# First transfers in quarters, and the last normalisation shared by VectorE, ScalarE and GpSimd with stores in halves

## The reference, cut to what matters

```python
def layer_norm(x, g, b):
    mu = xf.mean(-1, keepdims=True)
    var = jnp.square(xf - mu).mean(-1, keepdims=True)
    return (xf - mu) * lax.rsqrt(var + LN_EPS) * g + b

for l in range(DEPTH):                       # DEPTH = 2
    mix = hybrid_mixer(x, mem, w_in[l], ..., w_mem_kv[l], w_out[l], cos, sin)
    x = layer_norm(DEEPNORM_ALPHA * x + mix, ln1_g[l], ln1_b[l])
    ffn = moe_ffn(x, ...)
    x = layer_norm(DEEPNORM_ALPHA * x + ffn, ln2_g[l], ln2_b[l])

km, vm = jnp.split(mem @ w_mem_kv, 2, axis=-1)   # inside hybrid_mixer
```

## Time and profile before

| | us |
|---|---|
| median of 3 runs | 1241.95 |
| profiled execution, whole time | 1242.17 |
| its span (first to last instruction of the core) | 1240.2 |
| PE busy | 1199.5 |
| DVE busy | 426.9 |
| ACT busy | 335.4 |
| POOL busy | 10.4 |

### The profile page before, as it was taken

The page is one execution under the profiler, slowest core; times in us unless marked ns, Lnnn a source line. Parts: engine busy times, 40 slices in busy tenths (PEclk is TensorE's granted clock), DMA queues, the critical chain, the costliest instruction groups (busy, mean ns, idle before and its releaser), DMA issues.

```text
span 1240.2 us, 18632 instructions
## 1 busy us (share of the span) xinstructions
PE 1199.5 (97%) x8032; PEld 550.5 (44%) x8032; DVE 426.9 (34%) x1198; ACT 335.4 (27%) x637; POOL 10.4 (1%) x20
## 2 busy tenths in 40 slices
PE   7999899999999999999899999999999999999994
PEld 5764443333443334433386645344333443334431
DVE  0433732332333323333334336233333333333335
ACT  0132222322223222233212323222232222322221
POOL 0000000000000000000010000000000000000001
PEclk9999999999999999999999999999999999999998
DMA  9962389999999999999967405899999999999990
GB/s 390 417 282 80 103 358 435 424 435 425 432 424 427 429 432 429 432 426 433 423 248 309 193 35 221 362 429 430 430 433 427 431 429 428 429 429 428 429 400 37
DMA packets 26713, 452.48 MB, mean 365 GB/s; under 512 B 2944, under 2 KB 3072, under 8 KB 5504
## 3 DMA queue, kind: packets, MB, share of 16 engines
q1 hardware_dynamic: 26624, 451.21, 86.1%
HBM read 450.15 MB, written 1.05 MB: 364 GB/s over the span
## 4 chain that ended last, share of the span: by engine, by line
PE 95%; DVE 3%; DMA 1%; ACT 1%; issue 0%; POOL 0%; SPq 0%; POOLq 0%
PE bank L596 36%; PE bank L622 18%; PE bank L517 8%; PE bank L542 7%; PE bank L678 4%; PE bank L750 4%; PE bank L687 2%; PE bank L608 2%; PE bank L877 1%; PE bank L697 1%; PE bank L566 1%; PE bank L707 1%; PE bank L652 1%; PE bank L646 1%; PE bank L529 1%; DMA slots<-in_dense 1%
## 5 line engine op out<-in xcount | busy, mean ns | idle before, releaser
L622 PE MATMUL bank<-slots,scratch 128*32 128x512 f32 x2048 | 233.0, 595 | 2.3 <-issue 2.3
L596 PE MATMUL bank<-slots,xT 128*64 128x512 f32 x1024 | 226.1, 594 | 1.0 <-ACT xT L912 1.0
L596 PE MATMUL bank<-slots,scratch 128*64 128x512 f32 x1024 | 226.0, 594 | 0.0
L1183 DVE SCALAR_TENSOR_TENSOR scratch<-bank,small,scratch 128x512 f32<-128x512 f32 x128 | 96.1, 751 | 248.7 <-ACT scratch L912 248.7
L912 ACT ACTIVATE scratch<-bank,small 128x512 bf16<-128x512 f32 x128 | 87.9, 687 | 159.0 <-PE bank L622 159.0
L912 ACT ACTIVATE scratch<-bank 128x512 f32<-128x512 f32 (+2 forms) x122 | 67.0, 562 | 236.0 <-PE bank L517 76.9
L517 PEld LDWEIGHTS bank<-scratch 128*128 128x128 bf16 x1536 | 107.7, 146 | 50.4 <-issue 49.7
L596 PEld LDWEIGHTS bank<-slots,xT 128*64 128x64 f32 x1024 | 69.3, 137 | 130.6 <-issue 129.3
L596 PEld LDWEIGHTS bank<-slots,scratch 128*64 128x64 f32 x1024 | 69.2, 137 | 129.4 <-issue 129.4
L517 PE MATMUL bank<-scratch 128*128 128x128 bf16 x1536 | 117.1, 227 | 0.3
L622 PEld LDWEIGHTS bank<-slots,scratch 128*32 128x32 f32 x2048 | 60.8, 109 | 121.1 <-issue 117.1
(11 more groups left out here) (125 smaller groups left out, 697.2 us busy)
## 6 DMA issues: line engine op xcount, KB each, us to landing
slots<-in_w_gu SPq DMA_DIRECT2D x64, 4096.0 KB, 22.6
slots<-in_w_dn SPq DMA_DIRECT2D x64, 2048.0 KB, 20.9
slots<-in_dense SPq DMA_DIRECT2D x32, 1024.0 KB, 11.3
r<-in_pool_mat SPq DMA_DIRECT2D x2, 1024.0 KB, 19.7
r<-in_ln_g SPq DMA_DIRECT2D x4, 512.0 KB, 4.5
r<-in_ln_b SPq DMA_DIRECT2D x4, 512.0 KB, 5.9
slots<-in_shared_dn SPq DMA_DIRECT2D x2, 1024.0 KB, 4.9
scratch<-in_memt SPq DMA_DIRECT2D x2, 512.0 KB, 6.8
```

The lines of the kernel that those rows point to most:

```text
L596: m = pe.matmul(H[64 * a:64 * a + 64, :], xg[B % 2][:, k, j, a, :], GU[g][:, a, :, k, :], start=k == 0, stop=k == KD - 1)
L622: m = pe.matmul(Y[half][r0:r0 + 32, :], hT[:, kc * P + 64 * a + 32 * t:kc * P + 64 * a + 32 * t + 32], DN[g][:, a, kc, half * 512:(half + ...
L1183: dve.scalar_tensor_tensor(yres[:, half * 512:(half + 1) * 512], Y[half][:, :], wslot[:, b:b + 1], ysp[:, 0, half * 512:(half + 1) * 512], ...
```

## The change

At the start, the first layer's memory tokens and key and value weights are transferred in four quarters each (rows of 2 KB and of 4 KB), with a semaphore for each quarter. PE waits at k = 0, 2, 4 and 6 instead of at k = 0 and 4. The second layer keeps its halves. The count that PE waits for on later chunks of that buffer is adapted.

At the end, DVE runs the first pass (subtract mean, times gain) over both tiles without a wait for `rstd`. The second pass over tile 1 stays on DVE, in two halves of 512 columns. For tile 0 ScalarE multiplies by `rstd` in two halves, and GpSimd, behind its last `rstd` operation, adds the bias in two halves. SP stores four halves of 256 KB: tile 1's first, then tile 0's.

```diff
-                for h in range(2):
+                for i in range(4 if l == 0 else 0):
+                    a, z = i * KD * S // 4, (i + 1) * KD * S // 4
+                    sp.dma_start(mt[:, a:z], memt[:, a:z]).then_inc(first_in[i], 16)
+                    a, z = i * W_CHUNK // 4, (i + 1) * W_CHUNK // 4
+                    sp.dma_start(r[:, a:z], dense[l, 0][:, a:z]).then_inc(first_in[i], 16)
+                for h in range(2 if l else 0):
...
-            for t in range(NT):
-                sp.wait_ge(*x_at(DEPTH - 1, 1, t))
-                sp.dma_start(out[0, t * P:(t + 1) * P, :], xs[:, t, :]).then_inc(out_done, 16)
-            sp.wait_ge(out_done, 16 * NT)
+            for t in (1, 0):
+                for h in range(2):
+                    sp.wait_ge(out_rd[t], h + 1)
+                    a, z = h * D // 2, (h + 1) * D // 2
+                    sp.dma_start(out[0, t * P:(t + 1) * P, a:z], xs[:, t, a:z]).then_inc(out_done, 16)
+            sp.wait_ge(out_done, 16 * 2 * NT)
...
-                        if j == 0 and k % 4 == 0:
+                        if l == 0 and j == 0 and k % 2 == 0:
+                            pe.wait_ge(first_in[k // 2], 32)
+                        if l and j == 0 and k % 4 == 0:
...
+            act.wait_ge(centred, 1)
+            act.wait_ge(rstd_rd, 4 * DEPTH - 1)
+            for h in range(2):
+                v = xs[:, 0, h * 512:(h + 1) * 512]
+                copy(v, v, scale=rstd[:, 0:1]).then_inc(scaled, 1)
...
-                for t in range(NT):
-                    normalised(l, 1, t)
+                if l < DEPTH - 1:
+                    for t in range(NT):
+                        normalised(l, 1, t)
+                else:
+                    dve.wait_ge(ln_in, 64 * l + 64)
+                    for t in range(NT):
+                        dve.wait_ge(var_rd, 4 * l + 2 + t + 1)
+                        m = dve.scalar_tensor_tensor(xs[:, t, :], xs[:, t, :], mv[:, t, 0:1], lng, ALU.subtract, ALU.mult)
+                        m.then_inc(centred, 1)
+                    dve.wait_ge(rstd_rd, 4 * l + 4)
+                    dve.wait_ge(centred, 2)
+                    for h in range(2):
+                        v = xs[:, 1, h * 512:(h + 1) * 512]
+                        dve.scalar_tensor_tensor(v, v, rstd[:, 1:2], lnb[:, h * 512:(h + 1) * 512], ALU.mult, ALU.add)\
+                            .then_inc(out_rd[1], 1)
...
+            for h in range(2):
+                v = xs[:, 0, h * 512:(h + 1) * 512]
+                pool.wait_ge(scaled, h + 1)
+                pool.tensor_tensor(v, v, lnb[:, h * 512:(h + 1) * 512], ALU.add).then_inc(out_rd[0], 1)
```

More of the change, by code:

```diff
@@ L294, in build @@
         out_done = sem("out_done")
+        first_in = [sem(f"first_in{i}") for i in range(4)]
+        centred = sem("centred")
+        scaled = sem("scaled")
+        out_rd = [sem(f"out_rd{t}") for t in range(NT)]
         class Pass:
@@ L508, in chunk_wait @@
                 for h in halves:
-                    pe.wait_ge(chunk_in[c % 3][h], 48 * l + 16 * (c // 3) + 16)
+                    pe.wait_ge(chunk_in[c % 3][h], 48 * l + 16 * (c // 3) + (16 if c % 3 else 0))
             def gather(ps, B, quarter, buf, to=G):
@@ L642, in _ @@
                     for k in range(KD):
-                        if j == 0 and k % 4 == 0:
+                        if l == 0 and j == 0 and k % 2 == 0:
+                            pe.wait_ge(first_in[k // 2], 32)
+                        if l and j == 0 and k % 4 == 0:
                             chunk_wait(l, 0, (k // 4,))
-                            pe.wait_ge(memt_in[k // 4], 16 * l + 16)
+                            pe.wait_ge(memt_in[k // 4], 16)
                         m = pe.matmul(o[:, j * S:(j + 1) * S], W[0][:, k, j * P:(j + 1) * P], memT[l][:, k, :],
```

## The result

| | before | after |
|---|---|---|
| median of 12 runs, us | 1242.05 | 1246.06 |
| profiled execution, whole time | 1242.17 | 1245.75 |
| its span | 1240.2 | 1243.6 |

The ratio of the times is 1.0035, with a 95% interval of 1.0026 to 1.0043. By the medians the change made the kernel 4.0 us slower, and 1246.06 lies outside the stated range of 1239.9 to 1244.0.

The account below looks back on a forecast made before the run. PE bounds the kernel, leaving only its two ends: start -0.25 us (0.65 - 0.9) and end +0.4 (+1.0 - 0.6) sum to +0.15, 1242.3 us profiled, 1242.1 us timed; 8-in-10 range 1239.9 to 1244.0 us.

Parts of the forecast that it names:

- What bounds the kernel: Whole kernel: PE is busy 1199.5 of 1240.2 us, so only some 13 us at the start and 15 at the end decide.
- The store, -0.6 us: End: the last store is 256 KB instead of 512, saving 0.6 us; the other three are done or hidden by then.
- a sign of being wrong: End, profile after: POOL's additions under 0.8 us each, or DVE's second half as the last to end.
- The landing, +0.65 us: Start: smaller rows, more packets; the last quarter lands 0.65 us later, at some 13.5 us.
- the second rival: Start: a 2 KB packet costs as much as 4 KB, landing 2.9 us later; whole +2.4, 1244.4 us; chance 0.12.
- The work behind the landing, -0.9 us: Start: four fewer PE instructions of 227 ns remain behind the last landing, saving 0.9 us.
- the third rival: Start: TensorE still at the 1.2 GHz pace when the last quarter lands; whole +1.55, given as 1243.7 us; chance 0.06.
- the net of the start: Start: later landing less the shorter work behind it, 0.65 - 0.9 = -0.25 us, between -0.9 and +2.0.
- DVE and POOL, +1.0 us: End: POOL's additions (1.2 us each) take turns with DVE's halves; compute ends at 1238.15 us, 1.0 later.
- ScalarE off the path: End: ScalarE's two copies of 0.63 us are done by 1234.1 us and wait for POOL.
- Slower by over 0.2%: Whole kernel: a time over 1244.4 us, needing half of one rival or two small losses together; chance 0.07.
- the forecast's +0.15: Whole kernel: sum of -0.25 us at the start and +0.4 at the end, on the profiled execution.

Follow-up runs that it names:

- e2: Kernel before with only the changed end (shared last normalisation, four stores, tile 1's first), start untouched; ratio 1.0007 (0.9997 to 1.0017).
- e3: e2 with SP's four stores reordered: first halves of tiles 0 and 1, then the second halves; ratio 1.0000 (0.9991 to 1.0010).
- e10: e2 with tile 0's two bias additions on DVE instead of POOL, tile 0 stored first; one run, no ratio; 14.3 us from last combine to end of span.
- e1: Changed kernel with the end of the kernel before, so only the quarters at the start; ratio 1.0010 (1.0000 to 1.0020).
- e4: e1 with PE waiting for quarters 0 and 1 together, then 2 and 3, as for halves; ratio 1.0018 (1.0009 to 1.0027).
- e5: Kernel before with 2 KB and 4 KB rows in four transfers, PE waiting for all at k = 0; one run, no ratio; last landing 13.39 us.
- e8: e1 with 34 small products on zeros on PE ahead of the first quarter; one run, no ratio; last landing 14.95 us, 20 instructions behind it 4.58 us.
- e7: e2 with DVE's halves of tile 1 waiting for POOL's additions, tile 0 stored first; one run, no ratio; addition 1.24 us, DVE half 0.71 us alone.

## Why the prediction was wrong, point by point

**What bounds the kernel**: right. In these two profiles the whole difference lies at the two ends. (Other pairs differ by up to 1.6 us in between.)

**The store, -0.6 us: the step that failed most.** It said "The other three stores are issued earlier and are done or hidden by then". The sum for compute already had DVE's and POOL's instructions interleaved, but I did not carry their order over to SP's, which stood in the diff: tile 1's halves first. That order is right only if POOL ends last, as the forecast had it. DVE's second half ended last, which the prediction had listed as a sign of being wrong, and it held back two finished stores. Measured: +1.43 us in place of -0.6 (+0.75 in e2), and e3 took back 1.3 us by the order alone. In e3 and e10 the smaller last store does bring its gain: 2.5 and 2.6 us from DVE's end instead of 3.06.

**The landing, +0.65 us: mis-sized.** It was +1.47 in the profile after, and +0.9 and +1.1 in e1 and e4. The part from row size was about as worked out (0.4 to 0.7 in e5). By 4 us the changed kernel had moved 0.2 MB less (the sums of the windows), which is 0.5 us of transfer; the larger part was lost later. Packets between 3.0 and 3.5 us in before, after and e5, and then between 8 and 12 us in the same three:

```profile
DMA packets 26, 0.11 MB, mean 213 GB/s; under 512 B 0, under 2 KB 0, under 8 KB 26
DMA packets 25, 0.05 MB, mean 107 GB/s; under 512 B 4, under 2 KB 4, under 8 KB 25
DMA packets 66, 0.14 MB, mean 270 GB/s; under 512 B 0, under 2 KB 0, under 8 KB 66
DMA packets 244, 1.70 MB, mean 425 GB/s; under 512 B 29, under 2 KB 29, under 8 KB 46
DMA packets 459, 1.37 MB, mean 344 GB/s; under 512 B 49, under 2 KB 49, under 8 KB 445
DMA packets 464, 1.65 MB, mean 412 GB/s; under 512 B 32, under 2 KB 32, under 8 KB 425
```

Before and after look like the second rival's mechanism, as many packets in the same time at half the bytes. But e5, with the same small rows in four transfers, passed 66 of them in the first of these stretches and moved nearly as much as before in the second. So the time of a small packet is not what cost most; the rest came with the eight transfers (e1, e4 and e8 moved 1.45, 1.44 and 1.27 MB between 8 and 12 us), by a mechanism that no run here isolates.

**The work behind the landing, -0.9 us: given back by TensorE's pace.** This is the third rival, which had 0.06 (by its own +1.55 us its time should read 1243.5 and not 1243.7). The four instructions fewer are there, but 20 took 5.24 us where 4.54 (20 x 227 ns) were expected. I had argued that PE, beginning sooner, would be at full pace sooner, and that an idle 0.97 us had done no harm. Neither carried over to the changed kernel, where the work of the first quarters is followed by an idle 1.39 us and, after four more instructions, by another 0.31. e4 (waits for halves, full pace) and e8 (PE busy beforehand, full pace) show that it is PE's own past that decides. So the net of the start was +1.26 us and not -0.25.

**DVE and POOL, +1.0 us: right, with a smaller size.** They take turns, an addition costs 1.24 us where I took 1.2, and which of them starts did not matter for the sum (it did for the stores). DVE ended 0.68 us later than before. The difference to the forecast is that part of each instruction lies beside the other engine's (e7), and that the last to end is DVE and not POOL. The Trainium skill in "SBUF — State Buffer", section "Who interferes with whom", has the rule of turns, and the single instructions of e7 and after agree with it in the main (1.26 us beside, 1.24 alone for the first; 1.74 against 0.71 for the second), though the turns are not for quite the whole instruction: DVE's half ended 0.54 us after POOL's and takes 0.71 alone. The figure of the Trainium skill for GpSimd ("GPSIMD Engine Reference", section 3.1), by which an addition was estimated at 1.12 us in the prediction, is 0.12 us short of the 1.24 measured.

**ScalarE off the path**: right. It was done 0.2 us before POOL's first addition began (1235.43 against 1235.65).

**The chances.** Slower by over 0.2% had 0.07. Each of the three losses was named or had its place in the text, but they were priced as alternatives, while nothing kept them from coming together: +0.8 at the landing, +0.7 from the pace, +2.0 at the stores. Less 0.3 us by which the turns came out better, that is the 3.2 us between the forecast's +0.15 and the profile's +3.4.

Not settled: e1 and e2 add up to +0.17% and the whole change measured +0.35%. The intervals allow it only if the parts lie near their upper ends and the whole near its lower one; the sets were timed on different occasions. In the profiles the parts cost 0.84 and 1.4 us, 1.1 less than the two ends of the whole. Of that, 0.4 lies at the start and 0.7 behind DVE's end (the stores), where the code is the same in the part and in the whole.

## What to carry to other kernels

When a store queue serves several producers, work out in which order they will end and issue in that order: one late piece at the head of an in-order queue cost 1.3 us here, against 0.7 for the way in which the arithmetic was shared. Splitting a first transfer pays only if what is left behind the last landing gets shorter and the matrix engine stays busy in between. Here the split moved the landing back by 0.9 to 1.5 us where it could win 0.9, and thin work ahead of it left the engine at its slow pace. Losses that can happen at the same time belong in one sum, not in separate rivals.

## What the runs showed of the hardware

The joint between the layers decides 1.6 us by itself. There PE is nearly idle for some 3 us, and in some profiles the granted clock falls to the 1.2 GHz level right after it, in others not. The windows of the kernel before and of e3 (columns as in rows 4):

```profile
616.00:618.00 2.00, 2.00 (x7) 1.08 (x4) 1.15 (x2) 0.00 (x0) 0.00 (x0) 0.50 1.06 451
618.00:620.00 2.00, 2.00 (x8) 1.63 (x8) 1.97 (x5) 0.00 (x0) 0.25 (x2) 0.71 1.23 528
```

```profile
616.00:618.00 2.00, 2.00 (x12) 1.49 (x9) 1.55 (x3) 0.00 (x0) 0.00 (x0) 1.00 1.15 492
618.00:620.00 2.00, 2.00 (x11) 1.77 (x10) 1.97 (x5) 0.00 (x0) 0.66 (x2) 1.00 1.08 463
```
